# Half of the first block's modulation products leave the gated core, and the core's differences are written crosswise

## The reference

```python
for i in range(DEPTH):                      # 2 layers: 0 gated linear attention, 1 state space
    m_l = jnp.split((s_lat @ ada_w[i] + ada_b[i])[:, None, :], 6, axis=-1)   # latent
    m_c = jnp.split(s_ctx @ ada_w[i] + ada_b[i], 6, axis=-1)                 # context
    ...mixer(modulate(h, m[0], m[1])), gate m[2], layer_norm...
    ...sq_relu_mlp(modulate(h, m[3], m[4]), ffn_w1[i], ffn_w2[i]), gate m[5], layer_norm...
```

## Time and profile before

| | |
|---|---|
| median of 3 runs | 2619.12 us (2611.74 to 2620.15) |
| the profiled execution | 2622.63 us, span in the trace 2620.8 us |
| granted TensorE clock, mean | 0.972 of full speed |
| busy over the span | PE 94%, PEld 75%, DVE 52%, ACT 46%, POOL 24% |
| DMA | 302.15 MB, mean 115 GB/s |
| gated core | 197.3 to 361.2 us |
| layer 0's feed-forward part | from 452.6 us to about 795 us |
| layer 1's feed-forward part | from 1251.9 us |

### The profile page before, as it was taken

The page is one execution under the profiler, slowest core; times in us unless marked ns, Lnnn a source line. Parts: engine busy times, 40 slices in busy tenths (PEclk is TensorE's granted clock), DMA queues, the critical chain, the costliest instruction groups (busy, mean ns, idle before and its releaser), DMA issues. The chain is left out here.

```text
span 2620.8 us, 35297 instructions
## 1 busy us (share of the span) xinstructions
PE 2466.7 (94%) x13840; PEld 1973.1 (75%) x13840; DVE 1357.1 (52%) x2133; ACT 1203.8 (46%) x2062; POOL 618.4 (24%) x376
## 2 busy tenths in 40 slices
PE   6997989999999998899999999999999989989989
PEld 4784557888888887568999767577767877768778
DVE  2207657433444766437776534552566355454675
ACT  2824435422326433345654345564356233466364
POOL 2438610000006444110001442003401115502410
PEclk9998989999999999989999999999999999999999
DMA  6326853333324432564665231222321323324335
GB/s 234 90 79 236 289 163 85 108 97 97 97 81 118 110 87 81 193 209 137 178 185 153 73 95 47 60 65 70 81 65 51 103 73 96 110 77 114 87 95 145
DMA packets 416078, 302.15 MB, mean 115 GB/s; under 512 B 10211, under 2 KB 389193, under 8 KB 414889
## 3 DMA queue, kind: packets, MB, share of 16 engines
q1 hardware_dynamic: 414800, 299.45, 38.8%
q10 hardware_dynamic: 1112, 0.44, 0.1%
HBM read 298.80 MB, written 1.05 MB: 114 GB/s over the span
## 5 line engine op out<-in xcount | busy, mean ns | idle before, releaser
L217 POOL TENSOR_TENSOR weights_lo<-wslots,weights_hi 128x1024 fp32r<-128x1024 f32 x158 | 387.9, 2464 | 855.1 <-ACT weights_hi L207 854.5
L207 ACT ACTIVATE weights_hi<-wslots 128x1024 fp32r<-128x1024 f32 x398 | 418.0, 1054 | 275.3 <-PE psum L270 217.8
L270 PE MATMUL psum<-input_hi,weights_hi 128*128 128x512 f32 (+1 forms) x1400 | 501.8, 358 | 4.4 <-PEq L2931 1.8
L270 PE MATMUL psum<-input_hi,weights_lo 128*128 128x512 f32 (+1 forms) x1400 | 489.7, 350 | 0.0
L270 PE MATMUL psum<-input_lo,weights_hi 128*128 128x512 f32 (+1 forms) x1400 | 488.8, 349 | 0.0
L217 DVE TENSOR_TENSOR weights_lo<-wslots,weights_hi 128x1024 fp32r<-128x1024 f32 x240 | 296.8, 1244 | 183.9 <-ACT weights_hi L207 183.1
L270 PEld LDWEIGHTS psum<-input_hi,weights_hi 128*128 128x128 f32 x1400 | 264.6, 189 | 44.5 <-issue 7.5
L270 PEld LDWEIGHTS psum<-input_hi,weights_lo 128*128 128x128 f32 x1400 | 265.2, 189 | 37.8
L270 PEld LDWEIGHTS psum<-input_lo,weights_hi 128*128 128x128 f32 x1400 | 264.2, 189 | 38.9 <-issue 3.1
L270 PE MATMUL psum<-ffn_hidden_hi,weights_hi 128*128 128x512 f32 (+1 forms) x512 | 172.8, 338 | 0.0
L270 PE MATMUL psum<-ffn_hidden_hi,weights_lo 128*128 128x512 f32 (+1 forms) x512 | 172.5, 337 | 0.0
(11 more groups left out here) (481 smaller groups left out, 4910.7 us busy)
## 6 DMA issues: line engine op xcount, KB each, us to landing
wslots<-w_in SPq DMA_DIRECT2D x132, 512.0 KB, 4.0
wslots<-ffn_w SPq DMA_DIRECT2D x128, 512.0 KB, 4.0
wslots<-ada_w SPq DMA_DIRECT2D x80, 512.0 KB, 4.8
wslots<-ssd_w_in SPq DMA_DIRECT2D x49, 512.0 KB, 3.9
wslots<-w_ada SPq DMA_DIRECT2D x48, 512.0 KB, 4.5
wslots<-gla_w_in SPq DMA_DIRECT2D x25, 512.0 KB, 3.8
wslots<-w_br SPq DMA_DIRECT2D x24, 512.0 KB, 3.6
wslots<-ssd_w_out SPq DMA_DIRECT2D x16, 512.0 KB, 5.0
```

Source lines behind the costliest of these rows:

```text
L207: act.activation(self.part(self.whi_r, n), self.slot(n), ACT.Copy)\
L217: engine.tensor_tensor(self.part(self.wlo_r, n), self.slot(n), self.part(self.whi, n), ALU.subtract)\
L270: ins = pe.matmul(out_of(self.bank(g)), l, r, start=first and i == 0, stop=last and i == len(pairs) - 1, skip_group_check=not (first and l ...
```

## The change

1. Rounds 3 to 5 (layer 1's modulation, 48 slabs) leave the core. The 16 steps of rounds 1 and 2 stand after rounds 0 to 3 of each head.
2. A class `VectorSums` does these 48 slabs in layer 0's feed-forward part. SyncE loads each slab into one of two buffers of its own; VectorE multiplies it by the condition's column and adds it up for each of the two conditions (one multiply-add of 1024 columns each, eight slabs to a group, six groups); TensorE sums a group over the partitions with a matrix of ones (four products) and turns it (four transposes); ScalarE copies twice; GpSimd adds the bias. Slabs 0 to 15 go with the hidden tiles of the first half, 16 to 31 with its down slabs, 32 to 47 with the second half's tiles. The sums stand in `H2`.
3. Since `H2` is taken, the tokens `ctx_2` are loaded, turned (two tiles at a time after tiles 3 to 6) and copied in layer 1's feed-forward part, and the norm there comes up to three tiles later.
4. In the core VectorE makes both differences of a round, each written so that the query half and the key half land in the two rows of one side buffer (`crossed`); there are three side buffers. ScalarE makes two exponentials of full width, VectorE one product of 1024 columns with q and k. The hats' differences go into ScalarE's bias (eight exponentials of 128 per head in place of two of 512), and VectorE makes the hats' products, 1024 columns each. GpSimd keeps only the finishing of vectors.
5. Three pairs of semaphore names share a semaphore, and the gains of a layer norm wait for the shifted vectors.

```diff
-ADA_ROUND = {"ada_front": 0, "ada_core": 1, "ada_scan": 6}
+ADA_ROUND = {"ada_front": 0, "ada_core": 1, "ada_scan": 3}
...
-    ada("ada_core", [1, 2, 3, 4, 5])
+    ada("ada_core", [1, 2])
...
+class VectorSums:
...
+    def load(self, sp, upto):
+        b = self.b
+        for m in range(self.loaded, min(upto + 1, self.GROUPS * KD)):
+            if m >= 2:
+                sp.wait_ge(b.sem("vectors_added"), b.nth("vectors_added", 2 * (m - 1)))
+            g, k = divmod(m, KD)
+            sp.dma_start(self.ring[m % 2], b.dram["ada_w"][1][k * P:(k + 1) * P, g * SLOT:(g + 1) * SLOT])\
+                .then_inc(b.tick(f"slabs_in_{m % 2}", 16), 16)
+            self.loaded = m + 1
+
+    def add(self, dve, m):
+        b = self.b
+        g, k = divmod(m, KD)
+        dve.wait_ge(b.sem(f"slabs_in_{m % 2}"), b.nth(f"slabs_in_{m % 2}", 16 * (m // 2 + 1)))
...
+        for v in range(2):
+            acc, c = self.acc[:, g % 2, v, :], b.ada_c[:, 0, k, v:v + 1]
+            if k:
+                dve.wait_ge(b.sem("vectors_added"), b.nth("vectors_added", 2 * m + v - 1))
+                ins = dve.scalar_tensor_tensor(acc, self.ring[m % 2], c, acc, ALU.mult, ALU.add)
+            else:
+                ins = dve.tensor_scalar(acc, self.ring[m % 2], c, None, ALU.mult)
+            ins.then_inc(b.tick("vectors_added"), 1)
+
+    def sum(self, pe, g):
+        b = self.b
+        pe.wait_ge(b.sem("vectors_added"), b.nth("vectors_added", 2 * KD * (g + 1)))
+        for q in range(4):
+            ins = pe.matmul(b.psum[32 * q:32 * q + 32, self.SUM, :], b.ones[:, 0:32],
+                            self.acc[:, g % 2, q // 2, q % 2 * 512:(q % 2 + 1) * 512], start=True, stop=True,
+                            skip_group_check=True)
+        ins.then_inc(b.tick("group_summed"), 1)
...
+            SUMS = {(0, 10): 0, (0, HT + 3): 1, (0, HT + 10): 2, (1, 2): 3, (1, 10): 4, (1, HT + 2): 5}
+            TURNS = {(0, 11): 0, (0, HT + 4): 1, (0, HT + 11): 2, (1, 3): 3, (1, 11): 4, (1, HT + 4): 5}
...
                 if second:
+                    vectors.load(sp, 1)
+                else:
                     for t in range(2):
                         sp.dma_start(tok[:, t], b.dram["ctx_2"][0][t * P:(t + 1) * P].rearrange("p (k f) -> p k f", f=P))\
                             .then_inc(b.tick("tokens_in", 16), 16)
                 for i in range(2):
+                    if second:
+                        for j in range(HT):
+                            b.load(sp, ups[i][0] + j + AHEAD + RAW)
+                            vectors.load(sp, i * 2 * HT + j + 2)
                     b.stream(sp, f"ffn{l}_up{i}")
...
-                        if second and i == 0 and FIRST <= j < FIRST + KD:
-                            turn_tokens(j - FIRST)
...
+                        if not second and i == 0 and FIRST <= j < FIRST + KD // 2:
+                            turn_tokens(2 * (j - FIRST))
+                            turn_tokens(2 * (j - FIRST) + 1)
...
+                        if second:
+                            vectors.add(dve, i * 2 * HT + j)
...
-        STEPS = [1, 1, 1, 2, 2, 2, 1]
+        STEPS = [1, 1, 1, 1, 0, 0, 0]
...
+        def crossed(x, start, step, s, stride=None):
+
+            return bass.AP(x.tensor, x.offset + start, [x.ap[0], [step, 2], [2 * s, T // (2 * s)], [stride, s]])
+
+        def make_diffs(dve, q):
...
+            if q >= DEEP:
+                p = q - DEEP
+                dve.wait_ge(b.sem("score_made"), b.nth("score_made", p // NL * NI + p % NL + 2))
+            o = sides[:, q % DEEP, 0, :]
+            for z in range(2):
+                x = cum[:, z, h, :]
+                ins = dve.tensor_tensor(crossed(o, (1 - z) * s, T + (2 * z - 1) * s, s, 1),
+                                        crossed(x, (1 - z) * s, (2 * z - 1) * s, s, 1),
+                                        crossed(x, s - 1 + z, 0, s, 0), ALU.subtract)
+            ins.then_inc(b.tick("diffs_ready"), 1)
...
+                    act.wait_ge(b.sem("diffs_ready"), b.nth("diffs_ready", q + 1))
+                    act.activation(ak[:, q % DEEP, :], ak[:, q % DEEP, :], ACT.Exp, scale=-INV)
+                    act.activation(bq[:, q % DEEP, :], bq[:, q % DEEP, :], ACT.Exp, scale=INV)\
+                        .then_inc(b.tick("factors_ready"), 1)
...
                         dve.wait_ge(b.sem("factors_ready"), b.nth("factors_ready", q + 1))
-                        x = ak[:, q % 2, :]
-                        dve.tensor_tensor(x, x, kT[:, h, :], ALU.mult).then_inc(b.tick("key_side"), 1)
+                        x = sides[:, q % DEEP]
+                        dve.tensor_tensor(x, x, qk[:, h], ALU.mult).then_inc(b.tick("sides_ready"), 1)
...
+                        if q + DEEP - 1 < Q:
+                            make_diffs(dve, q + DEEP - 1)
+                        if n == 3:
+                            hats(h)
```

249 lines of the change are left out of this document (142 added, 107 removed).

## The result

| | before | after |
|---|---|---|
| median of the timed runs, us | 2619.6 (2611.7 to 2626.7) | 2583.5 (2579.3 to 2584.9) |
| ratio, 95% interval | | 0.9861 (0.9835 to 0.9887) |
| span of the profiled execution, us | 2620.8 | 2581.0 |

A forecast was written before the change was run, and what follows sets the result against it. It took TensorE's queue with its slabs to bound the core; -30 (core) + 8.8 + 2.5 - 2.2 (first feed-forward part) + 1.6 + 2.7 (second) = -16.6 us, from 2619.1 to 2602.5, written as 2603 us, range 2587 to 2619.

The forecast's parts named there:

- The core's sum: Gated core: VectorE's work of 122 us plus 12 us allowed makes 134 us, 30 us less than before.
- The allowance: Gated core: 12 us for head outputs holding TensorE's queue, head boundaries and a slower clock at the start.
- waits near 2 us: Gated core, rival of more gain: waits near 2 us instead of 12, total 2593 us; chance 0.10.
- The round: Gated core, VectorE: one 1024-column product 1.22, one copy 0.73, two differences 1.36, less overlapping starts, taken as 3.15 us.
- The differences at 0.68 in the crosswise pattern: Gated core, VectorE: each crosswise difference of 512 columns costs 0.68 us, within bounds of 0.68 and 1.14.
- Clock rival: Gated core: granted clock falls to 0.72, core only 16 us shorter, total 2617 us; chance 0.18.
- the prediction's own sign: Gated core: a granted clock below 0.96 would speak for the rival in which the clock eats the gain.
- GpSimd beside VectorE: Gated core: two-input operations stretch when both engines meet, a 512-column product from 0.68 to 1.52 us, not always blocked whole.
- First feed-forward part: Layer 0's feed-forward: sums and turns 8.8 us, start stall 2.5, token turns leaving 2.2; stage 9 us longer.
- the rival that has it fall behind: First feed-forward part: at 1.8 us per VectorE add, about 10 us late, total 2613 us; chance 0.06.
- the start stall: Start of the first feed-forward part: TensorE waits 2.5 us (0 to 5) behind the first slab's adds and a weight split.
- Second feed-forward part: Layer 1's feed-forward: token turns add 1.6 us and the wait for their loads 2.7 us (0 to 3.5).

The follow-up runs named there:

- cross_five: The kernel before with the new core's crosswise differences and three side buffers, all five modulation rounds kept in the core and feed-forward parts as before: 2620.1 us, ratio 1.0013.
- old_two: The changed kernel with the old core, VectorE and GpSimd sharing differences, products and hats, but only two modulation rounds in it: 2595.5 us, ratio 0.9924 to before.
- two_deep: The changed kernel with two side buffers in place of three: 2619.8 us, ratio 1.0009 to before; core 152.2 us.
- hats_pool: The changed kernel with the eight products of the hats moved from VectorE to GpSimd: 2587.9 us, ratio 0.9878 to before; core 120.6 us.
- early_tokens: The changed kernel with the loads of ctx_2 issued one stage earlier, in the layer norm stage: 2577.9 us, ratio 0.9858 to before; second feed-forward part 178.3 us.
- after_again: The changed kernel run once more, nothing changed: 2577.5 us, ratio 0.9856 to before.
- adds_only: The changed kernel without TensorE's six sums and turns in the first feed-forward part, VectorE's adds and the loads kept: 2573.2 us; that part 341.8 us.

## Why the prediction was right or wrong, point by point

- *What bounds the core before: right.* TensorE's queue with its slabs, not the rounds: cross_five takes 103 us of GpSimd's 107 out of the core and gains nothing, old_two takes 24 steps with their slabs' waits out and gains 37 us.
- *TensorE's work afterwards, 92 us: right* (92.3), and no slab waits, as costed.
- *The core's sum is the step that failed: 134 us forecast, 113.5 measured.* These 20.5 us are as much as the whole miss of 19.5; what else went otherwise (-9.0 in the state-space stages, -1.3 behind the core, +2.7 and +4.7) nearly cancels. The path was the right one, VectorE's. Its terms: 12 us allowed for TensorE's waits, where VectorE waited 1.8 us; 27 rounds at 2.94 instead of 3.15 us, 5.7; from the last copy to the end 8.5 instead of 10.7, 2.2; the start 7.6 instead of 9.0, 1.4; these three are 9.3 of it, the allowance less the 1.8 us is 10.2, and 1.0 is left for hats and states. The allowance treated every lump of TensorE's (4.6 us of outputs against a round of 3.15) as lost to VectorE. But differences and exponentials run a round ahead with three buffers, and rounds 4 to 6 of a head hold no steps, so TensorE catches up (in part argued: two_deep shows what the third buffer is worth, no run moved the steps of rounds 4 to 6 alone). The case "waits near 2 us" was in the text, as a rival with a small chance; the trace of before had no row for an undisturbed TensorE behind three buffers, and I put the allowance nearer to the old kernel's behaviour than the sum of the parts bore out.
- *The round: 3.15 forecast.* Product 1.22, copy 0.72, differences 0.68 each were right to 0.01; the overlap of their starts was 0.1 us at each of four starts, not at some.
- *The differences at 0.68 in the crosswise pattern: right* (0.676).
- *Clock rival: its mechanism occurred, its price did not.* The granted clock was 0.77 from 200 to 210 us, 0.72 from 210 to 220 and 1.00 behind, 0.95 over the core. By the prediction's own sign (below 0.96) that speaks for this rival, but the sign was a poor one: before itself has 0.96, and 0.72 from 210 to 220. Since VectorE is the path, scores at the lower level still fit in a round. The Trainium skill's warning (TensorE: Matmul & The Clock Gate, HAM oscillation) shows in single cases at other places, not again and again: behind the 3.60 us wait of the second feed-forward part (0.91 from 1201 to 1221) and behind the long slab wait in the state-space core (0.83 over the 20 us from the first step in before).
- *GpSimd beside VectorE: the price was read rightly from the earlier trace rows, what lies behind it was not.* The prediction says that the trace shows a lengthening and not always a whole block. Put GpSimd's operations of before beside VectorE's, and it is a block: the products of 219.00 and 222.14 in the earlier trace rows end 0.54 and 0.55 us behind these two of GpSimd, where alone they take 0.68.

```profile
218.49 1.49 POOL L1394 TENSOR_TENSOR gla_diff<-gla_cum 128x512 f32<-128x512 f32 x1
221.62 1.49 POOL L1394 TENSOR_TENSOR gla_diff<-gla_cum 128x512 f32<-128x512 f32 x1
```

They look merely stretched because they were issued when GpSimd's was half done. hats_pool shows the same with 1024 columns, eight times over. The rule of the Trainium skill (SBUF — State Buffer, Who interferes with whom) holds in these rows. The 14.2 us of VectorE for 25.3 us of GpSimd are no rate for other kernels: they depend on how far GpSimd's operation has come when VectorE's is issued.
- *First feed-forward part: right in sum, +8.7 against +9.1, by two errors that cancel.* The sums and turns cost 1.6 us a group instead of 1.46, 9.8 against 8.8; VectorE's adds took 1.278 us (1.28 forecast), so the rival that has it fall behind never came near; VectorE was busy for 245 us instead of some 255, since the first of each eight slabs has a plain multiply of 0.746 us; the start stall was 0.6 instead of 2.5: the first slab was there 2.6 us after VectorE asked for it (at 405.3), the two multiplies took 1.4 us together, and the split that TensorE waits for followed at 406.65.
- *Second feed-forward part: +7.0 against +4.3.* The turns cost less than the 1.6 forecast: early_tokens has them without the wait, and its stage is 0.7 us longer than before's (0.5 to 1.4 against three of the four profiles of that code). The wait was 3.6 instead of 2.7; and the lower clock behind it, some 1.7 us (4.84 against 3.17 for a tile), was not in the sum. early_tokens shows the two together: 6.3 us.
- *Costed at nothing and not nothing: the state-space steps, -5.4 us (-3.4 in after_again),* by the shift of a load of instructions. This can't be read from the change, but it belongs in the range: it is worth 3 to 6 us either way in that stage, though no total here showed it.

## What to carry to other kernels

Price a pipeline by the busy time of the engine that will be the path, and then ask of each lump of the others whether buffers run far enough ahead to swallow it: an allowance for waits needs a mechanism, and with one more buffer (here 38.7 us of it) there may be none. Halves of a change that give nothing, or little, one by one (0 and some 20 to 24 us here) can give 36 together, so a bound is only gone when all that share it are gone. Where VectorE is the path, look at which GpSimd operation is under way when each of its two-input operations is issued, and not at the mean price. And a wait of TensorE can cost more than its length: the one of 3.60 us was followed by some 1.7 us lost to the granted clock, so move the load that it waits for to the stage before.

## What the runs showed of the hardware beyond that

- A row of one to 64 elements taken crosswise with steps of both signs runs on VectorE like a plain one: 665 to 693 ns for 512 f32 columns in 56 instructions, against 0.68 us for a plain one.
- Loads of instructions share the DMA engines with the data. Where one of 16 KB fell on the first slabs of a burst, one slab's wait was 2.6 to 3.7 us instead of 1.1 to 1.3, in four profiles of four, and the stage up to 5 us longer, clock included.
- VectorE's f32 product of 1024 columns took 1.21 us with GpSimd idle and up to 3.07 beside a product of GpSimd (2.94 to 3.36 us each, their own waits included): it ended 1.08 to 1.09 us behind GpSimd's end. One of 512 columns (0.68 us alone) ended 0.54 to 0.55 us behind. A predicated copy from PSUM was not delayed.
- TensorE kept 350.5 of 351.6 us busy at clock 1.00 while VectorE added 48 slabs beside it: the two don't hinder each other by more than about 1 us there (adds_only against before).
